# One more Strassen pair in the first feed-forward, and a norm whose pieces are computed one slot earlier

## The reference, cut to what matters

```python
    hn = rmsnorm(x, ffn_norm_g)
    gu = hn @ w_up                                    # 1024 x 5632
    h = silu(gu[..., :2816]) * gu[..., 2816:]
    x = x + h @ w_down                                # 2816 x 1024
    return rmsnorm(x, final_norm_g)                   # end of the first block
...
    x = layer_norm(x, ln0_g, ln0_b)                   # start of the second
    h = x * (1.0 + sc_a) + sh_a
    proj = h @ w_in_2
```

## Time and profile before

| what | us |
|---|---|
| median of 3 runs (3452.5 to 3454.06) | 3452.77 |
| the profiled execution | 3456.12 |
| its span, first to last instruction | 3454.4 |
| PE busy (97% of the span) | 3359.9 |
| DVE busy (57%) | 1957.9 |
| ACT busy (38%) | 1306.3 |
| POOL busy (13%) | 440.2 |

### The profile page before, as it was taken

How to read it: one execution, slowest core, us unless ns; L and a number is a source line. 1 busy time by engine, 2 the same in 40 slices (tenths; PEclk the granted TensorE clock), 3 DMA queues, 4 the chain that set the end, 5 groups by cost and what they waited for, 6 DMA issues and landing times.

```text
span 3454.4 us, 39383 instructions
## 1 busy us (share of the span) xinstructions
PE 3359.9 (97%) x16072; PEld 2741.8 (79%) x16072; DVE 1957.9 (57%) x2420; ACT 1306.3 (38%) x1828; POOL 440.2 (13%) x321
## 2 busy tenths in 40 slices
PE   8999999999999899999999999999899999999998
PEld 6888888877877688888888877787698778888886
DVE  8454462333745435687872274444565778888326
ACT  4232111444155523433331156343434454444213
POOL 0000000000000000444440010000000015544000
PEclk9999999999999999999999999999999999999999
DMA  3313341113400024232347322220203322233831
GB/s 121 75 52 114 106 162 65 50 50 96 162 32 28 25 70 134 86 110 110 115 147 305 108 81 99 68 92 31 98 1 129 122 86 110 110 110 134 323 104 49
DMA packets 114964, 351.51 MB, mean 102 GB/s; under 512 B 16072, under 2 KB 26056, under 8 KB 114768
## 3 DMA queue, kind: packets, MB, share of 16 engines
q1 hardware_dynamic: 112672, 348.66, 28.8%
q10 hardware_dynamic: 2112, 0.33, 0.1%
HBM read 264.81 MB, written 82.95 MB: 101 GB/s over the span
## 4 chain that ended last, share of the span: by engine, by line
PE 86%; DVE 7%; ACT 6%; issue 1%; DMA 0%; ACTq 0%; SPq 0%; DVEq 0%
PE PS L498 44%; PE PS L2466 21%; PE PS L481 8%; PE PS L3883 1%; PE PS L3895 1%; PE PS L1930 1%; PE PS L1952 1%; PE PS L1622 1%; PE PS L516 1%; PE PS L996 1%; ACT dS L1678 1%; ACT whi L438 0%; PE PS L3888 0%; PE PS L1597 0%; DVE wlo L443 0%
## 5 line engine op out<-in xcount | busy, mean ns | idle before, releaser
L443 DVE TENSOR_TENSOR wlo<-raw,whi 128x1024 fp32r<-128x1024 f32 (+3 forms) x380 | 482.0, 1269 | 401.5 <-ACT whi L438 398.8
L438 ACT CAST whi<-raw 128x1024 fp32r<-128x1024 f32 (+3 forms) x380 | 359.1, 945 | 693.7 <-PE PS L498 342.4
L498 PE MATMUL PS<-xhi,whi 128*128 128x512 f32 x1872 | 603.3, 404 | 12.8 <-DVE sbVt L2148 6.3
L498 PE MATMUL PS<-xlo,whi 128*128 128x512 f32 x1872 | 581.1, 392 | 0.0
L498 PE MATMUL PS<-xhi,wlo 128*128 128x512 f32 x1872 | 579.0, 391 | 0.0
L498 PEld LDWEIGHTS PS<-xhi,whi 128*128 128x128 f32 x1872 | 345.8, 189 | 98.9 <-issue 14.0
L498 PEld LDWEIGHTS PS<-xlo,whi 128*128 128x128 f32 x1872 | 353.4, 189 | 75.4
L498 PEld LDWEIGHTS PS<-xhi,wlo 128*128 128x128 f32 x1872 | 352.6, 188 | 75.5
L2466 PE MATMUL PS<-tf,whi 128*128 128x512 f32 x936 | 288.4, 389 | 0.0
L2466 PE MATMUL PS<-xhi,whi 128*128 128x512 f32 x624 | 243.8, 391 | 2.5 <-DVE xlo L2451 2.5
L2466 PE MATMUL PS<-xlo,whi 128*128 128x512 f32 x624 | 243.8, 391 | 0.0
(11 more groups left out here) (589 smaller groups left out, 5589.7 us busy)
## 6 DMA issues: line engine op xcount, KB each, us to landing
raw<-in_w_up SPq DMA_DIRECT2D x88, 512.0 KB, 3.3
hid<-hs SPq DMA_DIRECT2D x88, 512.0 KB, 3.6
raw<-in_w_in SPq DMA_DIRECT2D x67, 512.0 KB, 3.3
slot<-hid SPq DMA_DIRECT2D x56, 512.0 KB, 6.6
adr<-in_w_ada SPq DMA_DIRECT2D x48, 512.0 KB, 4.7
raw<-in_w_down SPq DMA_DIRECT2D x40, 512.0 KB, 3.6
raw<-in_w_gate SPq DMA_DIRECT2D x32, 512.0 KB, 3.3
merged<-hid SPq DMA_DIRECT2D x16, 512.0 KB, 13.3
```

Source lines behind the costliest of these rows:

```text
L438: act.e.copy(whis[place(i)][:, ks, :], raws[i % RING][:, ks, :]).then_inc(*give("w_hi", i))
L443: dve.e.tensor_tensor(wlos[place(i)][:, ks, :], raws[i % RING][:, ks, :], whis[place(i)][:, ks, :].bitcast(F32), ALU.subtract).then_inc(*g ...
L498: ins = pe.e.matmul(ps[:, h * 512:(h + 1) * 512], w[s][:, k, :], x[:, h * 512:(h + 1) * 512], start=(at == 0 and n == 0), stop=(at == kt - ...
```

## The change

`PLAIN` goes from (2, 3) to (1, 3): pair 1 of feed-forward 1 becomes a Strassen pair, the 21st. Its input sums move from POOL to DVE, after the first scaling, and are split 4, 3, 2 instead of 3, 2, 4. In the norm, `ln0_var_dve` goes ahead of the weights of slot 4, and each `ln0_lo_dve` goes from the start of slot n+2 to the end of slot n+1, behind the running sum. The list `fast` is set anew at each start of the Strassen pairs, the pair of banks that was taken longest ago first. The functions `input_sums`, `sum_hi`, `sum_lo`, `ln0_var_dve` and `ln0_lo_dve` themselves stay as they are.

```diff
-PLAIN = (2, 3)
+PLAIN = (1, 3)
@@ SHARED
-    "sums_dve": "x_add sq_add t1_sum sum1 t2_sum t_sum2",
+    "sums_dve": "x_add sq_add t1_sum sum1 t2_sum t_sum1 t_sum2",
-    "sums_pool": "w_sum t_sum1 sv_w sv_c22 t1_add",
+    "sums_pool": "w_sum sv_w sv_c22 t1_add",
@@ as_banks
+            fast[:] = [6, 7] + [2 * p + x for p in dense for x in range(2)]
@@ ffn_pool
-            if f == 1:
-                input_sums(pool, 1)
@@ ffn1_act
-            for j in (3, 2, 4):
+            for j in (4, 3, 2):
                 sum_hi(act, 1, j)
@@ ffn1_dve
                 dve.e.tensor_tensor(FSG[i % 2], psum.of(j), rstd1, ALU.mult).then_inc(*give("f1_gate", i))
+                if i == 0:
+                    input_sums(dve, 1)
                 j = begin_dve(dve, "w_up", 22 + i)
                 if i == 0:
-                    for x in (3, 2):
+                    for x in (4, 3):
                         sum_lo(dve, 1, x)
                 dve.wait_ge("prod", j)
                 dve.e.tensor_tensor(FUV[i % 2], psum.of(j), rstd1, ALU.mult).then_inc(*give("f1_val", i))
                 if i == 0:
-                    sum_lo(dve, 1, 4)
+                    sum_lo(dve, 1, 2)
@@ ffn1_dve, last part of w_down
+                    if hf and ft == TOTAL:
+                        ln0_var_dve(dve, 0)
                     j = begin_dve(dve, "w_down", ft, k0)
...
+                    for k in SCALED.get(ft - 1, ()) if hf else ():
+                        ln0_lo_dve(dve, k, 0)
@@ ln0_first_dve
             elif slot == TOTAL:
-                ln0_var_dve(dve, 0)
                 ln0_factor_dve(dve, 0)
             for k in SCALED.get(slot, ()):
                 ln0_scale_dve(dve, k, 0)
-            for k in SCALED.get(slot - 2, ()):
-                ln0_lo_dve(dve, k, 0)
@@ ln0_second_dve
-            ln0_lo_dve(dve, 6, 0)
-            ln0_lo_dve(dve, 7, 0)
             ln0_mu_dve(dve, 1)
```

## The result

The changed kernel takes 3462.38 us, the median of 20 executions (3454.62 to 3472.59); the kernel before took 3454.62 beside it (20, 3452.5 to 3458.76). The ratio is 1.0018, 95% interval 1.0012 to 1.0024. The forecast was 3455.6 us with a range of 3450 to 3460: the median lies outside.

A forecast was written before the change was run, and what follows sets the result against it. PE, busy for 97% of the span, was taken as the bound. Pair +6.2 us and norm -3.4 us summed to +2.8 on the median of 3452.77, so 3455.6 us; range 3450 to 3460 over all, the forecast's own 3453.5 to 3458.

The forecast's parts named there:

- Part 1, the wait: Pair 1 of feed-forward 1: PE waits 0.5 us at p4 and 6.2 us at p5, for split 1.
- the -2.7: Pair 1 of feed-forward 1: 84 matmuls in place of 96 save PE 2.7 us.
- Part 1, the low clock: Behind the wait at p5, the clock falls and costs 2.2 us (1.75 to 2.7); part 1 in all +6.2 us.
- Part 2: Norm: earlier variance and splits shorten PE's waits, -3.4 us; bounds -7.0 and -1.6.
- five waits of PE: Norm: waits of 0.6, 1.15, 1.8, 0.9 and 0.5 us, together 4.9 in place of 8.2 us lost.
- The three hits: Norm, slots 5, 6, 7: DVE's splits and POOL's additions exclude each other, about 1.2 us each; without them 3.6 us lower.
- The sum: Whole kernel: +6.2 - 3.4 = +2.8 us, giving 3455.6 us, counted as the same; chance 0.55.
- the base: Median of the kernel before, 3452.77 us, on which the forecast put its +2.8 us.
- A: Norm: POOL's additions slip into gaps, no hits; -7.0 and 6.2 give 3452.0 us; chance 0.20.
- B: Pair 1: split 1 ready in time, no wait at p5; part 1 -2.2, 3443.6 to 3447.2 us; chance 0.06.
- C: Norm: clock stays low through several short waits, 5.5 us more; +8.3, 3461.1 us; chance 0.09.
- D: Norm wins nothing, since early splits hold back evacuation 7 and its sum; +6.2, 3459.0 us; chance 0.10.

The follow-up runs named there:

- block1_early: Changed kernel with the input sums ahead of the wait for the root and block 1 split straight behind blocks 4, 3, 2: 3455.10 us, 1.0003 to before.
- norm_no_pool: Changed kernel with POOL's additions of slots 5, 6 and 7 in the norm replaced by a one-column write: 3455.26 us, 0.9999 to before.
- both_fill5: Changed kernel with 5 matmuls in front of the delta stage's long wait and 24 in front of p5 of pair 1: 3460.64 us, 1.0015 to before.
- fill_both: Changed kernel with 18 added matmuls behind the delta stage's long wait and 24 meant to fill the wait for p5: 3473.32 us, 1.0063 to before.
- sums_early: Changed kernel with DVE's four input sums ahead of the wait for the root and block 4 cast before the first silu: 3455.11 us, 1.0001 to before.

## Why the sum was right and the time was not

*Part 1, the wait.* Right: 5.84 for 6.2, and 0.39 for 0.5. block1_early confirms the -2.7 as -2.68.

*Part 1, the low clock.* Right in kind, mis-sized, and one number where there are two. With the clock kept up, feed-forward is 641.93 - 637.80 = 4.1 us longer than before, where the sum had +4.0. With the clock falling it is 7.0 longer (644.75 to 644.84) or 5.5 (643.28 to 643.31): the low clock costs 2.8 to 2.9 or 1.4 us by the execution, not 2.2 (1.75 to 2.7). The part as a whole is +7.0 or +5.5 for +6.2.

*Part 2.* Right: -3.69 us (437.79 to 434.10) for -3.4, in all ten rows of the table with its edits and POOL's additions the same to 0.1. Its five waits of PE are there, in the order of the walk 0.27, 0.73, 1.56, 0.42 and 0.27 by the timeline for 0.6, 1.15, 1.8, 0.9 and 0.5: each was sized too long, and the total came out closer than its parts. The three hits cost 7.01 - 3.69 = 3.3 us for 3.6. The Trainium skill's rule of exclusion (SBUF — State Buffer, "Who interferes with whom") was the one by which the sum had them; the trace agrees, with 2.99 us for three splits beside POOL and 1.89 without.

*The sum.* +2.8 forecast; +3.3 or +1.8 by the stages (7.0 or 5.5, less 3.69), and only 1.7 between the two profiled spans, because the changed one began feed-forward 1 1.5 us earlier, in which the change has no part.

*Where it failed.* The step is "The sum", which puts +2.8 us on the median and so takes everything behind the norm to move as one block. It doesn't: the delta stage took 5.5 us longer than before in both traces of the upper group, and 0.1 to 0.2 less in the two of the lower. Of the 6.8 us between 3455.6 and 3462.38, 1.85 come from the base (3452.77 was a median of three; over 20 it is 3454.62). The other 4.9 are the median's step into the upper group (14 of 20 executions), whose two traces have 5.6 us more in that stage than the lower group's, 1.5 less in the pair, and a first row later by 3.1 and 4.5. That the whole group is so rests on these two traces, which aren't among the 20; for the 20 themselves only the mean granted clock is on record, lower in every one of the upper group. So the term that was put at nothing is the granted clock in stretches that the change doesn't touch, the delta stage first of all.

*The rivals.* A (no hits) and B (no wait at p5) are false here, and each came true when its condition was made: -7.01 in norm_no_pool, and no wait and 635.12 in block1_early. Against B the prediction said that nothing in the rows gives 6 us less on DVE. The earlier trace rows does: DVE stood idle for 5.92 us before the first scaling, and that is where block1_early puts the input sums. C is false in its place: the clock in the norm is 1.00, and the norm's stage is constant. Its mechanism, many short waits under which the clock doesn't hold, exists 400 us later. For that the prediction had named the Trainium skill's section on depth-cycling (TensorE: Matmul & The Clock Gate) and said that no row shows it; the rows of both_fill5, with 0.66 over 50 us at waits of at most 2.2, now do. D (the norm wins nothing) is false.

*What stays open.* What sets in one execution whether the clock falls in the delta stage, and whether the later start of that stage is a cause of it or only goes with it. The same page of the Trainium skill ("What's actually happening") says that the gate's windows run freely and aren't reset by the kernel's start; that would let equal waits end differently, as they do here, but no run could show the windows. Why the changed kernel has two clear groups and the kernel before has none (3452.5 to 3458.76) isn't explained either.

## What to carry to other kernels

Add up a change by stages between fixed instructions, and don't judge it by the whole: the stages gave +5.5 to 7.0 and -3.7 us, repeated to 0.15, while the median of the unaltered changed kernel was 3462.38 one time and 3458.15 another. With a stage of many short waits behind it, a delay of 1.8 us cost 5 in the median and one of 7.3 cost 12, though one of 3.65 cost only 4.3; so look there, at work that the change doesn't touch, before costing "moved by x" at x. A few matmuls whose result is overwritten, put in front of a long wait, can be worth more than the edit: here 5 of them took the norm's version from 0.9993 to 0.9973 (on two chips, each against the kernel before beside it); but they have to stand in the wait itself, be shorter than it, and need operands that are already there.

## What was not expected of the hardware

- The same instructions of the delta stage took 107.2 to 120.1 us, by the granted clock (1.00 to 0.65 from 2510 to 2550). With 113.05 us the waits were the same to 0.1; with 120.06 some were shorter (1.3 and 0.2).
- 8 repeated matmuls, 1.84 us of work, gave three of 11 executions 15 to 20 us above the fastest; 16 gave none.
- Behind a wait of 5.84 us the low clock cost 2.8 to 2.9 or 1.4 us. Behind one of 3.66 us it didn't fall (fill_both, 1.00 from 1412 to 1440), behind one of 3.56 us it did (sums_early, 0.56 from 1416 to 1423).
- A 128x512 matmul of float32 operands holds PE for some 0.9 us (5 of them, 4.46 us) where the split operands take 0.227.
